# Second stack's out-projection: the first halves of column groups 0 and 1 ahead of their second halves

## What is computed

```python
for l in range(DEPTH_2):
    u = rmsnorm_2(h, norm_w[l]).astype(x.dtype)
    proj = jnp.einsum('bsd,de->bse', u, w_in[l]).astype(f32)
...
    ml_out = mlstm_mixer(mqk, mv, mo, mg, mlstm_conv_w[l].astype(f32), mlstm_conv_b[l].astype(f32),
                         mlstm_gate_b[l].astype(f32), mlstm_norm_w[l].astype(f32)) * silu(mz)
    mix = jnp.concatenate([ret_out, diff_out, ssd_out, ml_out], axis=-1).astype(x.dtype)
    h = h + jnp.einsum('bse,ed->bsd', mix, w_out[l]).astype(x.dtype)
return rmsnorm_2(h, final_norm_w).astype(x.dtype)
```

## Time and profile before

| what | value |
|---|---|
| three executions | 2511.66, 2511.83, 2515.93 us |
| median | 2511.83 us |
| span of the profiled execution, first to last instruction | 2509.7 us |
| TensorE busy | 2317.7 us, 92% of the span, 11909 matmul records |
| VectorE busy | 1572.9 us, 63% |
| ScalarE busy | 750.7 us, 30% |
| GpSimd busy | 454.4 us, 18% |
| mean granted TensorE clock | 0.963 |

### The profile page before, as it was taken

One profiled execution on the slowest core, in us unless ns is written; L12 is line 12 of the kernel. 1 busy time (PEld: TensorE's weight loads), 2 busy tenths in 40 slices (PEclk: granted clock), 3 DMA queues, 4 the chain that ended last, 5 costly groups with the idle time before them and its releaser, 6 DMA issues.

```text
span 2509.7 us, 30480 instructions
## 1 busy us (share of the span) xinstructions
PE 2317.7 (92%) x11909; PEld 1752.3 (70%) x11909; DVE 1572.9 (63%) x2615; ACT 750.7 (30%) x1630; POOL 454.4 (18%) x625
## 2 busy tenths in 40 slices
PE   3989999999998999999899899999889999999987
PEld 2767777778776677777768665766667776657666
DVE  7576775773486666658655585846553647766473
ACT  2333312431014643342221433214121234232321
POOL 1203212420015532020200104012120000310130
PEclk6989999999999999999999999999999999999999
DMA  7440565053671014411212121221221211122111
GB/s 230 144 150 1 134 148 138 2 154 90 124 162 34 2 25 130 140 34 51 76 59 68 34 68 34 85 68 51 70 81 53 82 51 51 35 68 84 51 64 54
DMA packets 222545, 199.50 MB, mean 79 GB/s; under 512 B 85859, under 2 KB 205507, under 8 KB 222147
## 3 DMA queue, kind: packets, MB, share of 16 engines
q1 hardware_dynamic: 210883, 155.60, 22.1%
q0 software_dynamic: 11520, 41.95, 5.6%
HBM read 194.39 MB, written 2.10 MB: 78 GB/s over the span
## 4 chain that ended last, share of the span: by engine, by line
PE 71%; DVE 16%; ACT 5%; POOL 4%; issue 3%; DMA 2%; SPq 0%; DVEq 0%; ACTq 0%; POOLq 0%
PE bank L520 16%; PE bank L521 16%; PE bank L522 16%; PE bank L661 5%; PE bank L702 3%; PE bank L675 2%; PE bank L610 2%; DVE wring_parts L1592 2%; DMA mix<-in_ada_w 2%; POOL h_parts L2435 1%; DVE qb L2163 1%; DVE whi_parts L1591 1%; PE bank L814 1%; PE bank L947 1%; DVE bank L1710 1%
## 5 line engine op out<-in xcount | busy, mean ns | idle before, releaser
L521 PE MATMUL bank<-h_parts,whi_parts 128*128 128x512 f32 (+2 forms) x1248 | 500.4, 401 | 0.0
L1592 DVE TENSOR_TENSOR wring_parts<-wring,whi_parts 128x2048 fp32r<-128x2048 f32 (+1 forms) x126 | 283.6, 2251 | 4.3
L521 PEld LDWEIGHTS bank<-h_parts,whi_parts 128*128 128x128 f32 (+2 forms) x1248 | 234.0, 188 | 64.5 <-issue 5.9
L1591 DVE CAST whi_parts<-wring 128x2048 fp32r<-128x2048 f32 (+1 forms) x126 | 150.6, 1196 | 168.6 <-PE bank L522 144.1
L521 PE MATMUL bank<-mix_parts,whi_parts 128*128 128x512 f32 x512 | 202.4, 395 | 0.0
L520 PE MATMUL bank<-vt_parts,whi_parts 128*128 128x512 f32 (+2 forms) x456 | 192.0, 421 | 6.0 <-DVE wring_parts L1592 6.0
L522 PE MATMUL bank<-vt_parts,wring_parts 128*128 128x512 f32 (+2 forms) x456 | 182.3, 400 | 0.0
L1710 DVE CUSTOM_DVE_ANT_0 bank<-bank,causal 128x256 f32<-128x256 f32 (+3 forms) x256 | 120.5, 512 | 67.4 <-PE bank L661 65.8
L520 PE MATMUL bank<-pt_parts,whi_parts 128*128 128x512 f32 x368 | 155.1, 421 | 7.4 <-ACT kb L1188 5.3
L522 PE MATMUL bank<-mix_parts,wring_parts 128*128 128x512 f32 (+1 forms) x392 | 155.0, 395 | 0.0
L520 PE MATMUL bank<-mix_parts,whi_parts 128*128 128x512 f32 (+1 forms) x392 | 155.0, 395 | 0.0
(11 more groups left out here) (417 smaller groups left out, 4979.5 us busy)
## 6 DMA issues: line engine op xcount, KB each, us to landing
wring<-in_w_in SPq DMA_DIRECT2D x60, 1024.0 KB, 5.3
mix<-in_ada_w POOLq DMA_DIRECT2D x80, 512.0 KB, 4.6
wring<-in_w_out SPq DMA_DIRECT2D x16, 1024.0 KB, 5.2
wring<-in_mla_w_in SPq DMA_DIRECT2D x10, 1024.0 KB, 5.4
wring<-in_mla_w_out SPq DMA_DIRECT2D x8, 1024.0 KB, 5.1
wring<-in_swa_w_in SPq DMA_DIRECT2D x32, 256.0 KB, 4.6
wring<-in_nsa_w_in SPq DMA_DIRECT2D x32, 256.0 KB, 4.6
wring<-in_nsa_w_in SPq DMA_DIRECT2D x6, 1024.0 KB, 5.5
```

Of the source, the lines that this page charges most:

```text
L521: pe.matmul(bank, lh, rl, start=False, stop=False)
L1591: chain(dve.tensor_copy(high, whole))
L1592: dve.tensor_tensor(low, whole, high.bitcast(F32), ALU.subtract).then_inc(done, 1)
```

## The change

The order of the eight units becomes (0,0), (1,0), (0,1), (1,1), (2,0), (2,1), (3,0), (3,1), for the loads, the cuts and the matmuls alike. Blocks y0 to y3 have open sums at the same time, so y3 gets a bank of the ring `O` (two banks) in place of one of `V`. The four norm matmuls stay behind unit (0,0), now ahead of (1,0). On VectorE one `prepare()` moves: it now stands between the casts of chunks 8 to 11 and the four gate products, and the call behind y1's residual prepares one unit rather than two. The first stack's out-projection keeps its order (its function loses the arguments for the second stack).

```diff
+OUT_ORDER_2 = ((0, 0), (1, 0), (0, 1), (1, 1), (2, 0), (2, 1), (3, 0), (3, 1))
...
+        def y_ring(L, b):
+
+            return O if L >= 4 and b == 3 else V
+
...
-            for i in range(4):
-                for k in range(2):
-                    units.append(((4 + l, ("out", i, k)), out_unit(a["w_out_2"][l], UNIT * i, KC * k), whole))
+            for i, k in OUT_ORDER_2:
+                units.append(((4 + l, ("out", i, k)), out_unit(a["w_out_2"][l], UNIT * i, KC * k), whole))
...
+            def out_proj_2(L, means, norms):
+
+                b = {}
+                for i, k in OUT_ORDER_2:
+                    keys = [(L, "y", 2 * i + j) for j in range(2)]
+                    slots = by_chunk(weights(L, ("out", i, k)))
+                    if (i, k) == (1, 0):
+                        norms()
+                    if k == 0:
+                        for key in keys:
+                            b[key] = open_bank(y_ring(*key[::2]), key)
+                    steps = [(j, c) for j in range(2) for c in range(KC)]
+                    if i == 0:
+                        steps = [(j, c) for j in range(2) for c in range(4)] + [(j, c) for c in range(4, KC) for j in range(2)]
+                    for j, c in steps:
+                        at = k * KC + c
+                        if (i, k, j, c) == (0, 0, 0, 4):
+                            means()
+                        if i == 0 and j == 0:
+                            pe.wait_ge(*cnt(mix_split))
+                        mm = product(b[keys[j]][:, :], [t[:, c, j * P:(j + 1) * P] for t in slots],
+                                     (mix_high(L)[at], mix_parts[:, at, :]), at == 0, at == 2 * KC - 1)
+                        if at == 2 * KC - 1:
+                            mm.then_inc(y_ring(*keys[j][::2]).full, 1)
+                    if k == 0:
+                        mm.then_inc(out_half, 1)
+                        halves[0] += 1
+                        used((out_half, halves[0]))
+                    else:
+                        used(y_ring(*keys[1][::2]).filled(keys[1]))
...
             def residual(L, b):
-                dve.wait_ge(*V.filled((L, "y", b)))
-                bank = V.take((L, "y", b))
+                ring = y_ring(L, b)
+                dve.wait_ge(*ring.filled((L, "y", b)))
+                bank = ring.take((L, "y", b))
...
                 for c in range(8, 12):
                     mix_cut_high(c)
+                prepare()
                 for b in range(4):
                     chain(dve.scalar_tensor_tensor(out=mix[:, 12 + b, :], in0=qb[:, 4 + b, :], scalar=1.0, in1=qb[:, b, :],
...
                     if b % 2 and b < KC - 1:
-                        prepare(2)
+                        prepare(1 if b == 1 else 2)
```

More of the change, by code:

```diff
@@ L703, in causal_values, with out_proj @@
                 return mm
-            def out_proj(L, n_k, between=None, midway=None):
+            def out_proj(L):
                 for i in range(4):
                     keys = [(L, "y", 2 * i + j) for j in range(2)]
[L708 to L721, removed]
+                    slots = by_chunk(weights(L, ("out", i)))
+                    for j in range(2):
+                        bank = open_bank(V, keys[j])
+                        for c in range(KC):
                             if i == 0 and j == 0:
                                 pe.wait_ge(*cnt(mix_split))
[L724 to L731, removed]
+                            mm = product(bank[:, :], [t[:, c, j * P:(j + 1) * P] for t in slots], (mix_high(L)[c], mix_parts[:, c, :]), c == 0, c == KC - 1)
+                        mm.then_inc(V.full, 1)
                     used(V.filled(keys[1]))
@@ L952, in _ @@
                     attention(L, scores, values, fill)
-                out_proj(L, 1)
+                out_proj(L)
             for l in range(L2):
@@ L1158, in ml_norms @@
                         norm((L, "mo_", e), [pt[:, 0, e, :]])
-                out_proj(L, 2, ml_norms, ml_means)
+                out_proj_2(L, ml_means, ml_norms)
             norm_x(7)
@@ L1414, in _ @@
                 else:
-                    norm_x(L + 1, lambda k: V.emptied((L - 1, "y", k)))
+                    norm_x(L + 1, lambda k: y_ring(L - 1, k).emptied((L - 1, "y", k)))
                 for k in range(KC):
@@ L1565, in _ @@
                     decays()
-            norm_x(7, lambda k: V.emptied((5, "y", k)))
+            norm_x(7, lambda k: y_ring(5, k).emptied((5, "y", k)))
             for i in range(NT):
@@ L1773, in residual @@
                 else:
-                    dve.tensor_tensor(x[:, b, :], bank[:, :], x[:, b, :], ALU.add).then_inc(V.empty, 1)
+                    dve.tensor_tensor(x[:, b, :], bank[:, :], x[:, b, :], ALU.add).then_inc(ring.empty, 1)
             def weigh(b):
```

## The result

| | before | with the change |
|---|---|---|
| executions, us | 2511.66, 2515.93, 2511.83, 2518.18 | 2493.15, 2490.97, 2498.86, 2494.16 |
| median, us | 2513.88 | 2493.65 |
| span of the profiled execution, us | 2509.7 | 2491.4 |
| mean granted TensorE clock | 0.963 | 0.964 |

The ratio is 0.9924, 95% interval 0.9911 to 0.9937: about 19 us less than before, between 15.8 and 22.4 (the two medians differ by 20.2). The prediction was 2495.5 us, from 2493.0 to 2500.5.

The account below looks back on a forecast made before the run. TensorE was taken as the bound, standing still around the out-projection for late chunks and a late bank. From the profiled span, 2509.7 - 8.18 - 8.51 + 0.4 = 2493.4 us; plus 2.1 to the median gives 2495.5, range 2493.0 to 2500.5.

Parts of the forecast that it names:

- The bound and the gain from the gaps: Out-projection, norms to (2,0): TensorE's waits for chunks 12 to 15 and y0's bank go, 8.18 us (layer 5), 8.51 (layer 4).
- The shift of 3.5 us: VectorE: the moved cut delays chunks 12 to 15 by 1.22 + 1.06 + 3.23 - 2.05, about 3.5 us; bounds 1.5 and 5.5.
- The prediction's other sum: VectorE's moved cut: each instruction waits out a whole 1.48 us GpSimd subtraction, so the shift is 4.4 us, the kernel 2496.9.
- Chunks 12 to 15 in time: TensorE in (0,1): chunk 15 ready at 2421.2, wanted at 2422.2, one microsecond left; all four waits go.
- The cut of (1,1): VectorE's weight cut, the tightest place: ready 0.3 us before TensorE wants it in both layers; 0.2 us charged per layer.
- Loads, banks, ScalarE, and what is behind (2,0): Loads and banks off the path, ScalarE's work the same, TensorE from (2,0) on without a gap, moving up by the gain.
- The late cut: Rival: the cut of (1,1) comes late at TensorE, costing up to 2.0 us per layer, 2497.5 to 2499.5; chance 0.11.
- One stall kept: Rival: something behind the move in one layer eats that layer's gain, about 2503.5 us; chance 0.03.
- The waits only move: Rival: VectorE held at the moved cut by a late load, chunks 12 to 15 late again, 2511.8 us; chance 0.04.
- The clock: Rival: four open sums lower TensorE's clock to 1.2 GHz in (1,0) and (0,1), about 2531 us; chance 0.04.

Follow-up runs that it names:

- delay experiment: Two extra 128x512 VectorE additions (1.42 us in all) behind the gate products, added to the changed kernel; 2497.31 us in one run.
- sums in turn: Changed kernel with the sums of y2 and y3 taken in turns, product by product, in both units of group 1; 2492.61 us in one run.
- second experiment: Changed kernel with the moved cut behind the four gate products rather than ahead of them; 2495.13 us in one run.
- first, cuts behind chunk 15: Changed kernel with the cuts of (0,1) and (1,1) both behind chunk 15 on VectorE; median 2513.73 us against 2512.92 of the kernel before, ratio 1.0.
- fifth, layer 5 alone: Order, moved cut and bank changed in layer 5 only, layer 4 as in the kernel before; median 2504.66 us against 2513.24, ratio 0.9967.
- third, bank only: Kernel before with only y3's sum moved to a bank of ring O, old order and cuts; 2512.48 us in one run.
- the version with two more moved cuts: Changed kernel with prepare() also moved ahead of VectorE's wait in the SSD and mLSTM mixers; medians 2486.23 and, run again, 2489.22 us.

## Why the prediction was right

**The bound and the gain from the gaps: held.** The prediction read four late chunks and a late bank as the only thing that stops TensorE around this place, and worked out 8.18 and 8.51 us from the distance of an uninterrupted stream. The trace has 8.18 and 8.50.

**The shift of 3.5 us: held.** The multiplication for chunk 12 started 2405.11 - 2397.79 = 7.32 us behind the first norm matmul before, and 2398.76 - 2387.98 = 10.78 now: 3.46. Its terms were the cast with 1.06 on top (2.29, so 1.07), the subtraction of 3.23 (3.26), and a relief of 2.05 (4.90 fell to 2.86, so 2.04). The prediction's other sum, 4.4 us and 2496.9 for the whole, let each of the cut's two instructions wait out a whole GpSimd subtraction of 1.48. The rows of the change say what they waited for; GpSimd's third and fourth subtraction of chunks 8 to 11:

```profile
2390.11 1.45 POOL L2495 TENSOR_TENSOR mix_parts<-mix,vt_parts 128x512 fp32r<-128x512 f32 x1
```

```profile
2391.52 2.27 POOL L2495 TENSOR_TENSOR mix_parts<-mix,vt_parts 128x512 fp32r<-128x512 f32 x1
```

The cast starts at 2390.36, 1.20 us ahead of the end of the third, and takes 1.07 more than alone. The subtraction starts at 2392.68, 1.11 ahead of the end of the fourth, and takes 0.97 more. Behind chunk 15 it is the same: 1.12 left of GpSimd's at 2410.32, and 3.26 instead of 2.29. So each loses what is left of the GpSimd subtraction that runs when it starts, less about 0.14 us. And it goes both ways: the fourth subtraction takes 2.27 instead of 1.45, with the cast running until 2392.65. The Trainium skill (SBUF — State Buffer, "SBUF: two separate sides") calls the shared port pair an exclusive lock, on which the other engine fully blocks. The trace agrees with that; too high in the 4.4 was only the length of the waits.

**Chunks 12 to 15 in time: held.** No idle stands ahead of any of them.

**The cut of (1,1): the one term that was mis-sized.** The prediction gave it 0.3 us of slack and charged 0.2 per layer all the same. The slack was 0.23 in layer 5 and nothing was lost in either layer, so the 0.4 us of the sum wasn't there. The delay experiment shows that caution was in place, since 1.42 us more on VectorE cost 1.39.

**Loads, banks, ScalarE, and what is behind (2,0): held.** No wait on any of them appears in the stretch.

**The rivals.** The late cut: the mechanism exists, from 0.23 us on, and wasn't reached. One stall kept: layer 4 gained as much as layer 5, and changing layer 5 alone gave half. The waits only move: that is what the new order does when the cut stays behind chunk 15, but there the cut is late by its place in VectorE's stream, not by a late load, the only way that the prediction named for this kernel. The clock: 1.00 throughout, also with sums in turn.

**What the sum leaves over.** The span fell by 18.3 us, and the two distances by 16.7. Outside them, the start up to layer 4's norms is 0.53 us longer and the end 0.3 shorter. The remaining 1.84 is the stretch from unit (2,0) of layer 4 to the norms of layer 5, in which the program has the same instructions: 603.09 us before, 601.25 after. It is the clock. Two windows of this stretch, 340 to 380 and 500 to 520 us behind its start, of the kernel before:

```profile
2134.70:2174.70 40.00, 36.87 (x144) 25.71 (x143) 31.42 (x55) 9.62 (x21) 6.86 (x9) 0.91 0.12 34
2294.70:2314.70 20.00, 18.30 (x62) 12.01 (x62) 9.14 (x15) 4.09 (x10) 3.40 (x8) 0.83 0.17 52
```

And with the change:

```profile
2126.73:2166.73 40.00, 36.90 (x150) 26.09 (x149) 32.77 (x58) 10.27 (x22) 7.74 (x9) 0.96 0.15 44
2286.73:2306.73 20.00, 18.35 (x62) 11.13 (x60) 8.27 (x15) 4.30 (x10) 3.41 (x8) 0.91 0.17 52
```

A window of 20 us at 0.83 is one with about 7 us at 1.2 GHz. The clock is under 1.00 in three more windows of the stretch, and all five together have about 32 us at 1.2 GHz before and 28 with the change; 4 us at half the clock cost about 2. The starts of the stretch's 2631 matmul records drift apart between the two profiles in these five windows, and outside them by under 0.1 us. The other profiles fit within 0.7 us:

| profile | stretch, us | at 1.2 GHz, us |
|---|---|---|
| before | 603.09 | 32 |
| second experiment, cut behind the gate products | 602.94 | 32 |
| first, cuts behind chunk 15 | 601.88 | 28 |
| fifth, layer 5 alone | 602.95 | 31 |
| third, bank only | 605.04 | 35 |
| sixth, small delay | 604.52 | 35 |
| the change, its second profile, and sums in turn | 601.25, 601.18, 601.24 | 28 |

It doesn't follow the order of the units: the second and the sixth experiment have the new one and stand with the slower. One and the same kernel, the version with two more moved cuts, took 597.8 us there in one profile, with 24 us at 1.2 GHz, and 601.1 in the other, with 35; those 11 us more cost only 3.3, so part of such time costs nothing. Why a profile has more or less of this time stays open, and so does whether the change has a part in it.

So the whole time came out as forecast by the mechanism, but where in the range it fell is in part luck. 2493.65 is only 0.65 us above the range's low end, which had been given 1.5 us for such matmuls at half the clock; beside it, the same kernel measured again gave 2495.74, and the kernel before had 2513.88 this time, 2.1 more than the prediction was worked out from.

## What to carry to other kernels

Before reordering a matmul stream, work out how long it would be without gaps, then write down for every input when it is ready and when the new order wants it; here that gave the gain to 0.1 us. The reordering, the small work that starts the late chain (four norm matmuls, 6.6 us per layer by their place) and the preparation of the next weights ahead of that chain (without it, no gain at all) count as one edit. Preparation that an engine does at a fixed place in its stream is best placed where the engine would wait anyway, which gave 6.5 us more here.

## What was not expected of the hardware

- An idle of 7.35 us on TensorE was followed by about ten matmuls at a granted clock of 0.50, 0.43 us apart, and cost 2 us on top; the five idles of before, 1.12 to 1.91 us each and within 14 us, left the clock at 1.00.
- A VectorE instruction that starts beside a running GpSimd subtraction lost what was left of that one less about 0.14 us: 1.07 for 1.20, 0.97 for 1.11. So the loss was the same for either order of the gate products and the cut: 8.43 and 8.41 us for the same six instructions, some 2.05 of it loss.
- A wait of TensorE cost about 0.27 us more than its idle shows, for the restart: 0.64 us for 0.38, 0.76 for 0.49. So five short waits with 6.87 us of idle were worth 8.2.
